# Splitting the score matmuls of a page group into six parts that alternate with a prompt step and with four pages of weighted values, in a two-layer decoder step

## The reference, cut to what matters

```python
# sample group: 8 sequences, 12 heads of 64, 32 pages of 128 past rows each, gathered by page_table
s_past = einsum('bqhd,bkhd->bhqk', q, k_past) * scale + g[..., :, None] + suffix[..., None, :]
s_new  = einsum('bqhd,bkhd->bhqk', q, k) * scale + g[..., :, None] - g[..., None, :]   # causal
p = softmax(concatenate([s_past, s_new], -1))
out = einsum(p[..., :n_past], v_past) + einsum(p[..., n_past:], v)
# prompt group: 12 heads, 4 blocks of 128 queries
sc = einsum('bqhd,bkhd->bhqk', qb, k) * scale + cb[..., :, None] - cum[..., None, :]   # causal
out = einsum(softmax(sc), v)
```

## Time and profile before

| | us |
|---|---|
| median of 3 runs | 2256.04 |
| lowest and highest | 2252.41, 2258.34 |
| the profiled execution's own time | 2258.42 |
| its span, first to last instruction | 2256.5 |

### The profile page before, as it was taken

How to read it: one execution, slowest core, us unless ns; L and a number is a source line. 1 busy time by engine, 2 the same in 40 slices (tenths; PEclk the granted TensorE clock), 3 DMA queues, 4 the chain that set the end, 5 groups by cost and what they waited for, 6 DMA issues and landing times.

```text
span 2256.5 us, 41057 instructions
## 1 busy us (share of the span) xinstructions
PE 2010.6 (89%) x16827; PEld 1490.6 (66%) x16827; DVE 1052.1 (47%) x1915; ACT 344.1 (15%) x796; POOL 196.5 (9%) x260
## 2 busy tenths in 40 slices
PE   6999587787778666989999999999997899999996
PEld 3777355555555443767777777677775677777774
DVE  4441556666566554453334444223455533344443
ACT  2002122122212111012221000111011022210002
POOL 1400000000000000200001222000001000002220
PEclk9999789999999977999999999999898999999998
DMA  4210688888889898122222222312111122222221
GB/s 164 75 38 4 249 308 318 312 308 314 307 312 328 295 351 335 67 75 75 75 75 75 75 75 75 112 39 75 46 36 64 58 75 75 75 75 75 75 75 42
DMA packets 127606, 320.40 MB, mean 142 GB/s; under 512 B 9852, under 2 KB 10130, under 8 KB 127294
## 3 DMA queue, kind: packets, MB, share of 16 engines
q1 hardware_dynamic: 123874, 304.65, 37.2%
q0 software_dynamic: 3296, 12.98, 1.6%
q10 hardware_dynamic: 252, 0.16, 0.0%
HBM read 309.20 MB, written 8.55 MB: 141 GB/s over the span
## 4 chain that ended last, share of the span: by engine, by line
PE 86%; issue 4%; DVE 4%; DMA 2%; ACT 2%; SPq 1%; ACTq 0%; POOL 0%; DVEq 0%
PE ps L837 50%; PE ps L1023 7%; PE ps L1045 4%; PE ps L1140 3%; PE ps L1141 3%; PE ps L969 2%; PE ps L968 2%; PE ps L980 2%; PE ps L752 1%; PE ps L753 1%; ACT wring L1445 1%; PE ps L781 1%; PE ps L1032 1%; PE ps L992 1%; PE ps L782 1%
## 5 line engine op out<-in xcount | busy, mean ns | idle before, releaser
L837 PE MATMUL ps<-work 128*128 128x288 f32 x1152 | 294.8, 409 | 12.0 <-DVE work L1640 7.8
L837 PE MATMUL ps<-xn,wring 128*128 128x288 f32 x1008 | 268.9, 410 | 16.7 <-DVE xn L1593 15.7
L837 PEld LDWEIGHTS ps<-work 128*128 128x128 f32 x1152 | 220.6, 192 | 74.7 <-issue 13.4
L837 PE MATMUL ps<-big,wring 128*128 128x288 f32 x944 | 252.9, 412 | 7.6 <-DVE big L2141 7.6
L1857 DVE STREAM_TRANSPOSE work<-work 128x768 f32<-128x768 f32 x256 | 238.2, 957 | 39.2 <-DMA work<-in_cache_k 38.5
L837 PEld LDWEIGHTS ps<-xn,wring 128*128 128x128 f32 x1008 | 193.4, 192 | 71.8 <-issue 16.5
L837 PEld LDWEIGHTS ps<-big,wring 128*128 128x128 f32 x944 | 182.2, 194 | 59.4 <-DVE big L2141 8.5
L1023 PE MATMUL ps<-work,big 32*32 32x256 f32 x6144 | 149.1, 414 | 59.5 <-issue 43.4
L1667 DVE TENSOR_TENSOR work<-ps,work 128x288 f32<-128x288 f32 x72 | 33.0, 458 | 321.1 <-PE ps L837 321.1
L685 POOL TENSOR_TENSOR h<-h,xn 128x288 f32<-128x288 f32 x96 | 106.1, 1108 | 812.5 <-DVE xn L1674 697.7
L1045 PE MATMUL ps<-wring 128*32 128x192 f32 x2048 | 123.6, 384 | 48.1 <-ACT wring L1445 34.5
(11 more groups left out here) (346 smaller groups left out, 2458.1 us busy)
## 6 DMA issues: line engine op xcount, KB each, us to landing
work<-in_cache_k SPq DMA_DIRECT2D x256, 384.0 KB, 5.7
wring<-in_cache_v SPq DMA_DIRECT2D x256, 384.0 KB, 7.9
wring<-in_w_up SPq DMA_DIRECT2D x16, 2048.0 KB, 8.2
wring<-in_w_down SPq DMA_DIRECT2D x16, 2048.0 KB, 7.8
wring<-in_w_in_odd SPq DMA_DIRECT2D x6, 2048.0 KB, 8.1
wring<-in_w_in_even SPq DMA_DIRECT2D x5, 2048.0 KB, 9.0
big<-in_w_out_even SPq DMA_DIRECT2D x2, 2048.0 KB, 16.7
wring<-in_w_out_odd SPq DMA_DIRECT2D x2, 2048.0 KB, 8.6
```

The lines of the kernel that those rows point to most:

```text
L837: last = mm(bank, w[:, k, :], x[:, k, :], start=k == 0 and not onto, stop=k == 3, skip_group_check=onto)
```

## The change

`score_group(g)` is split. `score_part(g, n)`, n from 0 to 5, issues the 16 matmuls of one n (32 passes), with the group's waits in front of part 0. `add_bias(g)` adds the bias by four matmuls of 32x128 (weights `head_row`, 32 rows and 128 columns; 256 columns moved), one for each bank, in place of sixteen of 32x32; the wait for the turned bias goes with it. TensorE's order becomes: part 0, `prompt_step(2g)`, part 1, then page 4 of group g-1, part 2, page 5, part 3, page 6, part 4, page 7, part 5, the bias, `prompt_step(2g+1)`, `turn_probs(g)`, `weigh` where one is due, pages 0 to 3. ScalarE's and VectorE's order follow it: `maximum(2g)` and `divisors(2g)` come before `shift_group(g)`, `maximum(2g+1)` between page 3 and the bias, `divisors(2g+1)` between pages 5 and 6; one page is turned ahead of `maximum(2g)` and two behind it.

```diff
             def prompt_step(n):
-                if n >= NT + 1 and (n - 1) % NT == 0 and n <= NSTEP + 1:
-                    weigh((n - 1) // NT - 1)
                 if 1 <= n <= NSTEP:
                     turn(n - 1)
                 if n < NSTEP:
                     score(n)
 
-            def score_group(g):
+            def score_part(g, n):
                 b = g // GS
-                pe.wait_ge(sem("k_turned"), GP * (g + 1))
+                if n == 0:
+                    pe.wait_ge(sem("k_turned"), GP * (g + 1))
+                    pe.wait_ge(sem("queries_staged"), b + 1)
+                    if g:
+                        pe.wait_ge(sem("exp_done"), g)
+                    pe.wait_ge(sem("outputs_placed"), max(g - 1, 0) // GS)
+                for c in range(CG):
+                    for q in range(4):
+                        r = slice(32 * q, 32 * q + 32)
+                        mm(ps[32 * c:32 * c + 32, 4 + q, 0:256], qcur[r, b % 2, c, n // 2, n % 2, :],
+                           group_keys(q, g, 2 * HC * c + n), start=(n == 0), stop=False, skip_group_check=True)
+            def add_bias(g):
                 pe.wait_ge(sem("bias_turned"), g + 1)
...
+                for q in range(4):
+                    r = slice(32 * q, 32 * q + 32)
+                    last = mm(ps[:, 4 + q, 0:256], head_row[r, :], bias_T[r, g % 2, :], start=False, stop=True,
+                              skip_group_check=True)
                 last.then_inc(sem("scored"), 1)
@@ tensor, the loop over g
-                score_group(g)
+                score_part(g, 0)
+                prompt_step(2 * g)
+                score_part(g, 1)
+                for n in range(2, 2 * HC):
+                    if g:
+                        weigh_page(g - 1, GP // 2 + n - 2)
+                    score_part(g, n)
+                add_bias(g)
                 if g % GS == GS - 2 and new < NB:
                     turn_new(new)
-                if g:
-                    for p in range(GP // 2, GP):
-                        weigh_page(g - 1, p)
+                prompt_step(2 * g + 1)
                 if g % GS == GS - 2 and new < NB:
                     weigh_new(new)
-                prompt_step(2 * g)
                 turn_probs(g)
+                if g % 2 == 0 and 2 <= g <= 2 * H:
+                    weigh(g // 2 - 1)
                 for p in range(GP // 2):
                     weigh_page(g, p)
...
-                prompt_step(2 * g + 1)
@@ scalar
-                    exp_prompt(2 * g - 1)
-                if 0 <= 2 * g - 2 < NSTEP:
-                    take_turned(2 * g - 2)
-                exp_group(g)
-                if 1 <= 2 * g - 1 < NSTEP:
                     take_turned(2 * g - 1)
-                take_probs(g)
                 if 2 * g < NSTEP:
                     exp_prompt(2 * g)
+                exp_group(g)
+                if 2 * g < NSTEP:
+                    take_turned(2 * g)
+                take_probs(g)
+                if 2 * g + 1 < NSTEP:
+                    exp_prompt(2 * g + 1)
@@ vector
-                turn_pages(g + 1, range(0, 3))
-                if 1 <= 2 * g - 1 < NSTEP:
-                    divisors(2 * g - 1)
+                turn_pages(g + 1, range(0, 1))
+                if 2 * g < NSTEP:
+                    maximum(2 * g)
+                turn_pages(g + 1, range(1, 3))
+                if 2 * g < NSTEP:
+                    divisors(2 * g)
                 shift_group(g)
...
-                if 2 * g < NSTEP:
-                    maximum(2 * g)
+                turn_pages(g + 1, range(3, 4))
+                if 2 * g + 1 < NSTEP:
+                    maximum(2 * g + 1)
+                if g + 1 < NG:
+                    turn_bias(g + 1)
                 if g % 2 == 1 and g >= 3 and g // 2 - 1 < H:
                     head_out(g // 2 - 1)
-                turn_pages(g + 1, range(3, 4))
-                if g + 1 < NG:
-                    turn_bias(g + 1)
-                turn_pages(g + 1, range(4, 5))
-                if 2 * g < NSTEP:
-                    divisors(2 * g)
-                turn_pages(g + 1, range(5, 8))
+                turn_pages(g + 1, range(4, 6))
+                if 2 * g + 1 < NSTEP:
+                    divisors(2 * g + 1)
+                turn_pages(g + 1, range(6, 8))
...
-                if 2 * g + 1 < NSTEP:
-                    maximum(2 * g + 1)
```

More of the change, by code:

```diff
@@ L1003, in prompt_step @@
                     score(n)
-            def score_group(g):
+            def score_part(g, n):
                 b = g // GS
-                pe.wait_ge(sem("k_turned"), GP * (g + 1))
-                pe.wait_ge(sem("bias_turned"), g + 1)
-                pe.wait_ge(sem("queries_staged"), b + 1)
-                if g:
[L1012 to L1023, removed]
+                if n == 0:
[10 more added lines that the diff above has]
+            def add_bias(g):
+                pe.wait_ge(sem("bias_turned"), g + 1)
+                for q in range(4):
+                    r = slice(32 * q, 32 * q + 32)
+                    last = mm(ps[:, 4 + q, 0:256], head_row[r, :], bias_T[r, g % 2, :], start=False, stop=True,
+                              skip_group_check=True)
                 last.then_inc(sem("scored"), 1)
```

## The result

| | before | after |
|---|---|---|
| median, us (4 runs each) | 2255.31 | 2279.62 |
| lowest and highest of after | | 2278.14, 2288.28 |
| ratio, 95% interval | | 1.0116 (1.0087 to 1.0144) |
| span of the profiled execution | 2256.5 | 2276.8 |

The kernel is 1.2% slower. 2238 was predicted, with a range of 2200 to 2264: the sign is wrong and the time lies outside the range.

The account below looks back on a forecast made before the run. Neither DMA nor any engine was full, so waits were taken to bound the kernel. Groups 0.62 us shorter (25 times) and 0.4 us (6 times) made 18 us off 2256: 2238 us, range 2200 to 2264.

Parts of the forecast that it names:

- What TensorE's steps cost: TensorE's work in S: parts 3.9, pages 1.85, prompt step 2.44, bias 0.7, in all 8.9 us.
- S: Half of a group from part 0 to the end of the bias (`scored`): 8.9 us before pauses and lower clock.
- rival A: Changes of tile cost on top, or bias passes run one behind the other: 2265 to 2291 us; chance 0.19.
- The pauses: TensorE's waits in S when it has run out of instructions: 0.8 us a group, against 2.7 before.
- The lower clock: Cost of time at half clock, the 1.2 GHz level: 0.35 us a group, against 1.4, as few pauses reach 3 us.
- L: Half of a group from `scored` to the next part 0, the waits between scores: 9.5 us.
- VectorE's queue: VectorE's steps behind `scored` in an odd group: 9.8 us; even groups done earlier, the load setting about 9.1.
- ScalarE's moved steps: Steps moved on ScalarE, in its queue: 0.4 to 1.0 us each, due a whole S or L later.
- The bias: Four matmuls of 32x128 at the end of S: 0.7 us, taken near the lower end of 0.53 to 2.2.
- B: Keys' loop slower than 9.5 us or pauses stay at 2 us: no change, 2256; chance 0.16 together with D.
- D: Instructions aren't spread, as twelve loads in a burst slow each packet: B's number; chance 0.16 together with B.
- the copy's wait: Sign of a right forecast: the wait of TensorE's weighing for ScalarE's copy, 34.5 us before, halves.

Follow-up runs that it names:

- v3: Kernel before, with only pages 4 to 7 of the values set between the score parts, bias still in sixteen matmuls: 2275.24 us, 1.0097.
- v6: v2 with pages 4 to 7 back behind the scores and the prompt step 2g behind part 2: 2214.94 us, 0.9823.
- v1: Changed kernel with divisors(2g+1) on VectorE behind pages 6 and 7 instead of between 5 and 6: 2261.05 us, 1.0027.
- v4: Kernel before with only the bias changed, to four matmuls of 32x128, order untouched: 2228.99 us, 0.9885.
- v2: v1 with take_probs(g) ahead of take_turned(2g) on ScalarE: 2259.16 us, 1.0016.
- v8: v2 with pages 4 to 7 back behind the scores and the prompt step 2g behind part 0: 2236.07 us, 0.9912.
- v7: v2 loading only 64 of 128 rows of the second four pages of each group's keys, from the third group on: 2253.69 us, 0.9987.
- v9: v2 with VectorE's page 3, bias and head_out ahead of the maximum over the banks, page 4 ahead of the prompt's maximum: 2257.46 us, 0.9994.
- v11: v9 with v7's half loads of keys: 2250.15 us, 0.9970.
- v10: v6 with VectorE's order of v9: 2209.95 us, 0.9781.
- v12: v10 with the prompt step 2g in two pieces, turn behind part 1 and score behind part 3: 2221.73 us, 0.9851.
- v5: v3 with the bias in four matmuls of 32x128: 2259.28 us, 1.0016.

## Why the prediction was wrong, by its own steps

**What TensorE's steps cost: right.** A part was put at 0.65 us, a page on its own at 0.46, the bias at 0.7; the chain of after has 0.65, 0.46 to 0.48 and 0.69. In the six groups of after whose S has neither pause nor half clock, S took 9.1 us on average; the steps were summed to 8.9. So rival A, changes of tile that cost on top, is out: there are about 18 of them in a group, and each step lasts what it lasted in a run or what the earlier trace rows gave for it. The Trainium skill, TensorEngine Tiling (Array Packing), section Key Properties, says that a change of the tiling mode drains the engine; this trace shows no further cost of it than the 0.08 us by which a page between parts is longer than one in a row.

**The pauses: right.** 0.8 us a group was the sum, 0.88 is measured. That they exist at all still goes against what the Trainium skill's page Runtime: NRT & Kernel Launch says under Instruction fetch mechanics, that the fetch at a 16 KB boundary is mostly hidden. But the reason they fell isn't the pages. v3, with the pages alone, kept 2.02; v6, with the prompt step in the middle and no page in S, has 0.82. So in after and v6 I put it to the prompt step, 10 passes in 2.54 us in group 11 where a part has 32 in 0.65, that gives the queue time to catch up.

**The lower clock: wrong, 0.35 us for what is up to 1.15 in S alone.** I tied half clock to the pauses, since it stood behind one in the earlier trace rows, and let it fall with them. The pauses fell by two thirds and half clock stayed: 2.99 us a group against 3.15, of it 2.29 in S, where work at half speed costs half of that. It now begins behind the wait for the keys: before, 14 of its 15 stretches began just behind a pause of more than 1 us; in after 10 of 14 begin just behind TensorE's idle time of more than 1 us in front of part 0, and 2 behind a pause (just behind: within 5.5 us of the gap's start, a bound of mine for the count). In group 14 the first part takes 1.17 us, where group 11's took 0.73, and the turn of eight passes 2.00 where group 12's took 1.09. The rows are from the chain of after, then the window of the same stretch, columns as above, with a PEclk of 0.50:

```profile
553.17 1.17 PE ps L1015 x32
554.34 2.00 PE ps L980 x8
```

```profile
553.20:556.60 3.40, 3.40 (x41) 2.37 (x42) 0.50 (x3) 0.61 (x3) 0.00 (x0) 0.50 1.03 392
```

Together with the sum's other terms S was 8.9 + 0.8 + 0.35 = 10.05, and 10.58 is measured: 0.53 too little. The steps' 0.2 is the smaller part of it, half clock the larger.

**L: wrong, 9.5 for 10.21.** For odd groups VectorE's queue was summed to 9.8 and 9.41 is measured, so that step held. The one that failed is the sentence that ScalarE's moved steps are due a whole S or L later; the sum has no term for them. `take_turned(2g)` had been put ahead of the copy and behind the prompt's weighing, and the divisors that depend on it ahead of two pages. So even groups took 10.94 us where I had written 9.1. v1 shows it: with the divisors last, 18 us of 24 are gone.

**The sum.** 0.53 and 0.71 us too little are 1.24 in each of 25 groups, 31 us, and 0.94 in each of 6 later ones, 6 us. On the profiled execution's own time, 2258.4 - 18 + 37 = 2277, where after's is 2278.8. So the account closes on two mis-sized terms. But the larger error is ahead of them.

**The bias: wrong, and it hid the rest.** It was put at 0.7 us against 0.65, no gain. v4 shows a gain of 26 us. v4's interval puts the gain between 13 and 39 us. What was left, the new order, therefore cost about 2280 - 2229 = 51 us, where I had expected it to give 18. The runs split the 51: from after to v2, ScalarE's and VectorE's order, 20; from v2 to v8, the four pages out of S, 23; from v8 to v4, the prompt steps and the rest, 7, and there the intervals overlap.

**Why the order loses.** My cut into S and L was right, and I didn't follow it to its end. L has a floor that doesn't hang on TensorE: the load of keys from `scored` on and VectorE's queue, near 9 us. Before, TensorE's own work filled L to 12.7, so some of it could go. The change took 4 pages and a prompt step out, about 1.5 + 2.4 us, and L fell by 2.5, to where the floor and the detour hold it, with S longer by 3.1. v2 against v8 prices the pages: 1.85 us in S, 0.86 in L. v6 takes only the prompt step into S, where it breaks the run, and leaves the pages in the wait for the exponentials; with the cheaper bias it is the kernel whose S grew by 0.96 us and whose L fell by 2.58.

**The rivals.** B, that the keys' loop holds and TensorE waits for what it saved, came nearest in kind, but its time was 2256, and it had 0.16 together with D. D, that instructions aren't spread, is out by the pauses. A's times, 2265 to 2291, take in the measured 2280, but not for its reason: neither of its two costs is there. None of the four had the half clock of S in it. Of the signs named in advance the issue at the end of blocks, the wait for L1863 in front of part 0 and the clock that stayed at 0.93 are told above; the copy's wait, which should have halved, is 35.9 us against 34.5.

**What stays open.** Why half clock is 2.7 to 4.1 us a group in after, v1, v2, v7, v9 and v11, 2.9 in v8, and 1.2 to 1.7 in v6, v10 and v12. What TensorE did before it tells a part. In after, v1, v2, v7, v8, v9 and v11 the groups in front of whose part 0 TensorE stood idle for more than 1.5 us (my cut, no limit of the chip) have 2.8 to 4.6 us of half clock in S on average, the others 0.0 to 0.9. So the wait that the change opened in front of part 0 goes with it, though no run takes that wait alone away, and in v6, with 15 such groups, they have only 1.4. In v3, v5 and v11 the rest lies in L of even groups, and 23 of these three runs' 38 stretches begin just behind a pause. The three kernels with little half clock are those with the pages out of S and the prompt step amid the parts, whole or in two; the runs show that and not the reason. Nor is it known what makes up the 0.3 us of v4 beyond its pauses, though its half clock would be enough.

## What to carry to other kernels

When a cycle has a dense half and a half with a floor of its own, here a load and another engine's queue, work belongs in the waits of the second half up to its floor; only what is above the floor may move, and what moves should be few long instructions, as the prompt step here, behind which the instruction queue had caught up. When a step is moved on one engine, follow the queues of the other engines behind it one by one: "due much later" is true of the result and not of what stands behind the step. A wait that is opened in front of dense work may cost more than its length: here half clock went with it in seven of the kernels. And a change of two parts wants each part alone: the small one was worth 26 us here and covered half of what the large one lost.

## What the runs showed of the hardware that was not expected

- Four matmuls of 32x128 with 256 columns take 0.64 to 0.69 us for their eight passes, the same as sixteen of 32x32 in 32 passes (0.65). They save nothing in TensorE's time by the chain, and 48 instructions a group, with which the kernel was 26 us faster.
- A pause costs more than its length. In the chain of after, at 496.65, there are 0.22 us of issue in a part of group 11. The 24 passes ahead of it took 0.62 us and the 8 behind it 0.63, so that the part lasted 1.47 us instead of 0.65.
- Two limits on L within 0.4 us of each other: removing either gave 0.3 to 0.4 us in odd groups, removing both 1.4.
